# Seven half-width products for eight in the third feed-forward, and the high part of the gated product on ScalarE

## What is computed

```python
def swiglu(h, w_gu, w_down):                       # ffn2, D_FF = 2816
    a, b = jnp.split(h @ w_gu, 2, axis=-1)
    return (jax.nn.silu(a) * b) @ w_down

x = x + 0.5 * gt3[:, None, :] * swiglu(modulate(rms_norm(x, g_ffn2[l]), sh3, sc3), w2_gu[l], w2_down[l])
x = rms_norm(x, g_final)
...
h = rms_norm_2(x, ffn_norm_pre[l])                 # ffn3, D_FF_2 = 2816
y = swiglu_ffn(h, w_gate_up[l], w_down[l])         # (silu(g) * u) @ w_down
x = x + rms_norm_2(y, ffn_norm_post[l])            # the result
```

## Time and profile before

| | |
|---|---|
| median of 3 runs | 2179.72 us (2177.22 to 2183.71) |
| profiled execution | 2180.38 us, its span 2178.6 us |
| mean granted TensorE clock | 0.986 of full |
| TensorE busy | 2115.9 us (97%) |
| VectorE busy | 1297.3 us (60%) |
| ScalarE busy | 755.6 us (35%) |
| GpSimd busy | 57.1 us (3%) |

### The profile page before, as it was taken

How to read it: one execution, slowest core, us unless ns; L and a number is a source line. 1 busy time by engine, 2 the same in 40 slices (tenths; PEclk the granted TensorE clock), 3 DMA queues, 4 the chain that set the end, 5 groups by cost and what they waited for, 6 DMA issues and landing times.

```text
span 2178.6 us, 29042 instructions
## 1 busy us (share of the span) xinstructions
PE 2115.9 (97%) x11558; PEld 1769.7 (81%) x11558; DVE 1297.3 (60%) x2056; ACT 755.6 (35%) x1128; POOL 57.1 (3%) x34
## 2 busy tenths in 40 slices
PE   7999999999999999999999999998999999999998
PEld 6888888788887778788999987776688887888887
DVE  7766665644325874586877877775465465333335
ACT  4222212322323662432333354556443432212123
POOL 2000000000000000110000000000030000000000
PEclk9999999999999999999999999999999999999999
DMA  9555453222222112133222323310123122222222
GB/s 363 219 197 186 174 205 114 92 97 96 94 104 86 40 44 92 58 105 108 97 100 94 116 97 116 117 40 21 53 103 136 39 82 73 96 97 96 97 97 78
DMA packets 36452, 235.15 MB, mean 108 GB/s; under 512 B 4422, under 2 KB 6726, under 8 KB 8840
## 3 DMA queue, kind: packets, MB, share of 16 engines
q1 hardware_dynamic: 34988, 230.53, 29.1%
q10 hardware_dynamic: 1372, 3.37, 0.4%
HBM read 229.16 MB, written 4.72 MB: 107 GB/s over the span
## 4 chain that ended last, share of the span: by engine, by line
PE 86%; DVE 10%; ACT 2%; issue 1%; POOL 1%; DMA 0%; SPq 0%; DVEq 0%; ACTq 0%; POOLq 0%
PE ps L603 84%; PE ps L1018 2%; DVE w_lo L2388 1%; DVE s_lo L2396 1%; DVE ada_acc L2217 1%; ACT w_hi L1395 1%; DVE w_lo L2036 1%; DVE act_lo L2093 0%; POOL x L1989 0%; DMA ada_slot<-in_ada 0%; DVE raw L2412 0%; DVE normed L2105 0%; DVE hid_hi L2446 0%; ACT pt L1395 0%; DVE consts L2415 0%
## 5 line engine op out<-in xcount | busy, mean ns | idle before, releaser
L603 PE MATMUL ps<-act_hi,w_hi 128*128 128x512 f32 (+1 forms) x1744 | 669.4, 384 | 15.0 <-DVE s_lo L2396 4.0
L603 PE MATMUL ps<-act_lo,w_hi 128*128 128x512 f32 (+1 forms) x1744 | 658.8, 378 | 0.0
L603 PE MATMUL ps<-act_hi,w_lo 128*128 128x512 f32 (+1 forms) x1744 | 658.7, 378 | 0.0
L1395 ACT ACTIVATE w_hi<-raw 128x2048 fp32r<-128x2048 f32 (+4 forms) x205 | 340.3, 1661 | 333.6 <-PE ps L603 317.5
L603 PEld LDWEIGHTS ps<-act_hi,w_hi 128*128 128x128 f32 x1744 | 329.8, 189 | 87.1 <-issue 12.9
L603 PEld LDWEIGHTS ps<-act_hi,w_lo 128*128 128x128 f32 x1744 | 329.8, 189 | 61.2
L603 PEld LDWEIGHTS ps<-act_lo,w_hi 128*128 128x128 f32 x1744 | 330.1, 189 | 58.5 <-issue 1.0
L2036 DVE TENSOR_TENSOR w_lo<-raw,w_hi 128x2048 fp32r<-128x2048 f32 x133 | 304.9, 2293 | 62.3 <-ACT w_hi L1395 60.6
L603 PE MATMUL ps<-hid_hi,w_hi 128*128 128x512 f32 (+1 forms) x680 | 261.3, 384 | 1.7 <-DVE hid_lo L2542 1.7
L603 PE MATMUL ps<-hid_lo,w_hi 128*128 128x512 f32 (+1 forms) x680 | 260.1, 382 | 0.0
L603 PE MATMUL ps<-hid_hi,w_lo 128*128 128x512 f32 (+1 forms) x680 | 260.0, 382 | 0.0
(11 more groups left out here) (426 smaller groups left out, 2740.3 us busy)
## 6 DMA issues: line engine op xcount, KB each, us to landing
raw<-in_weights SPq DMA_DIRECT2D x176, 1024.0 KB, 4.8
ada_raw<-in_ada SPq DMA_DIRECT2D x30, 1024.0 KB, 4.9
ada_slot<-in_ada SPq DMA_DIRECT2D x6, 1024.0 KB, 14.6
bias_rows<-biasrow SPq DMA_DIRECT2D x8, 320.0 KB, 16.7
x<-in_x SPq DMA_DIRECT2D x1, 2048.0 KB, 8.2
table<-bias_rows ACTq DMA_DIRECT2D x1, 2048.0 KB, 9.2
result<-x SPq DMA_DIRECT2D x7, 256.0 KB, 2.1
consts<-in_consts SPq DMA_DIRECT2D x1, 1088.5 KB, 7.2
```

Source lines behind the costliest of these rows:

```text
L603: return nc.tensor.matmul(out, lhsT, rhs, start=start, stop=stop)
L1395: return nc.scalar.activation(out, in_, func, **kw)
```

## The change

- `ffn3` has its 18 blocks of `SEVEN` too and runs with `ffn_seven(2, ...)`. Its normed activations go to `act_full3` in place of the four `gained` buffers. The activation sums come after its second block (`turn` is 1). `ffn`'s look-ahead of one block becomes that of `ffn_seven`, two blocks.
- There is no room for all buffers: `t_hi3` lies over tiles 0 to 5 of x. ScalarE's queue copies these 1.5 MB to device memory (`kept`) once the last normed tile is there, and waits for that before it writes `t_hi3`; SP brings them back when TensorE is done with the last seven-product block, ahead of the loads of the last two weight blocks. The residual sums of the tail wait for it (`x_back`).
- `s_raw` is one buffer; `mix_weights(b)` waits for `split_lo` of b in place of b - 1. `s_lo31` lies where the second buffer was.
- `hid_hi` is written by ScalarE in both feed-forwards, after `s_hi` of b + 2 and once the product is there (`hid_high`); `hid_lo` comes after `s_lo` of b + 2 on VectorE.
- The activation sums are made by VectorE, in `ffn2` ahead of the loop, and `t_hi`, `t_lo` of `ffn2` in its first step in place of the second. GpSimd's four operations are gone.

The diff, cut to what matters (the rest hands `idx` and the buffers through):

```diff
--- before.py
+++ after.py
@@ -136,6 +136,8 @@
...
+        with ExitStack() as s:
+            t_hi3 = alloc(s, "t_hi3", [P, 3, 4, 256], F32R)
         x = sb("x", [P, DT, S])
@@ -163,6 +165,9 @@
...
+        with ExitStack() as s:
+            alloc(s, "consts_hole", [P, KAT["tri"]])
+            s_lo31 = alloc(s, "s_lo31", [P, 3, 4, P], F32R)
@@ -231,6 +236,18 @@
...
+        with ExitStack() as s:
+            alloc(s, "hid_hi_hole4", [P, 8, S]), alloc(s, "hid_lo_hole4", [P, 8, S])
+            alloc(s, "y_hole4", [P, DT, S])
+            with ExitStack() as t:
+                act_full3 = alloc(t, "act_full3", [P, DT, S])
+            t_lo3 = alloc(s, "t_lo3", [P, 3, 4, 256], F32R)
+            s_hi3 = [alloc(s, "s_hi30", [P, 3, 4, P], F32R)]
+            with ExitStack() as t:
+                t_raw3 = alloc(t, "t_raw3", [P, 3, 4, 256])
+            s_lo3 = [alloc(s, "s_lo30", [P, 3, 4, P], F32R), s_lo31]
+            s_hi3.append(alloc(s, "s_hi31", [P, 3, 4, P], F32R))
+            t1_raw3 = alloc(s, "t1_raw3", [P, 4, 256])
@@ -294,8 +311,12 @@
...
-        at = KAT["tri"]
-        s_raw = [spare[:], consts[:, at:at + 3 * S].rearrange("p (e t n) -> p e t n", e=3, t=4)]
+        s_raw = spare[:]
+        t_high_of, t_low_of = {1: t_hi, 2: t_hi3}, {1: t_lo, 2: t_lo3}
+        s_high_of, s_low_of = {1: s_hi, 2: s_hi3}, {1: s_lo, 2: s_lo3}
+        t_raw_of, t1_raw_of = {1: t_raw, 2: t_raw3}, {1: t1_raw, 2: t1_raw3}
+        full_of = {1: act_full, 2: act_full3}
+        kept = nc.dram_tensor("kept_x", (P, 6 * S), F32, kind="Internal").ap()
@@ -457,7 +479,7 @@
...
-        SEVEN = [AT["ffn2"] + 12 * third + j for third, n in enumerate(THIRDS)
+        SEVEN = [AT[name] + 12 * third + j for name in ("ffn2", "ffn3") for third, n in enumerate(THIRDS)
                  for j in range(4 if third == 0 else 0, n)]
@@ -584,9 +606,14 @@
...
-            with sp.Fori(AT["out2"] // 2, NB // 2) as p:
+            with sp.Fori(AT["out2"] // 2, NB // 2 - 1) as p:
                 for k in range(2):
                     next_load(p, k)
+            sp.wait_ge(x_kept, 16)
+            sp.wait_ge(block_done, done(SEVEN[-1]))
+            sp.dma_start(x[:, 0:6, :].rearrange("p t n -> p (t n)"), kept).then_inc(x_back, 16)
+            for k in range(2):
+                next_load(NB // 2 - 1, k)
@@ -658,15 +687,15 @@
...
                 pe.wait_ge(split_lo, b + 1)
-                pe.wait_ge(block_used, b + 1)
+                pe.wait_ge(block_used, b + 1 - offset)
...
-                pe.wait_ge(t_low, 3)
+                pe.wait_ge(t_low, 4 * idx - 1)
...
-                pe.wait_ge(t_low, 4)
+                pe.wait_ge(t_low, 4 * idx)
@@ -917,7 +946,7 @@
...
-                        if idx == 1:
+                        if idx >= 1:
                             plain = 2 if third == 0 else 0
@@ -1461,7 +1491,10 @@
...
-            def ffn_seven(b0, source):
+            def ffn_seven(idx, b0, source):
...
+                t_hi, t_raw, t1_raw = t_high_of[idx], t_raw_of[idx], t1_raw_of[idx]
+                s_hi, turn = s_high_of[idx], int(idx == 2)
...
                     p, k = divmod(b, 2)
...
                 def high_mixed(b):
                     if b in SEVEN:
                         act.wait_ge(s_step, 4 * nth(b) + 4)
-                        act.wait_ge(t_low, 3)
-                        fn(s_hi[b % 2][:], s_raw[b % 2]).then_inc(s_high, 1)
+                        act.wait_ge(t_low, 4 * idx - 1)
+                        fn(s_hi[b % 2][:], s_raw).then_inc(s_high, 1)
@@ -1489,10 +1522,11 @@
...
-                high(b0 + 1)
+                if idx == 1:
+                    high(b0 + 1)
                 for third, n in enumerate(THIRDS):
                     b = b0 + 12 * third
                     for j in range(n):
@@ -1506,8 +1540,12 @@
                         silu_of(b)
                         if more:
                             high_mixed(b + 2)
-                        if (third, j) == (0, 1):
-                            act.wait_ge(t_step, 4)
+                        act.wait_ge(block_used, used(b))
+                        fn(hid_hi[:, j, :], gu[b % 2][:, 0, :]).then_inc(hid_high, 1)
+                        if (third, j) == (0, turn):
+                            act.wait_ge(t_step, 4 * idx)
+                            if idx == 2:
+                                act.wait_ge(x_kept, 16)
                             for e in range(3):
                                 fn(t_hi[:, e], t_raw[:, e]).then_inc(t_high, 1)
                         b += 1
...
+                    elif idx == 2:
+                        token_tail(b, n)
@@ -1944,8 +1984,10 @@
...
-            prenorm()
-            ffn(AT["ffn3"], y, second_split=True, tail=True)
+            prenorm(full=act_full3)
+            act.wait_ge(x_ready, 3 * DT)
+            act.dma_start(kept, x[:, 0:6, :].rearrange("p t n -> p (t n)")).then_inc(x_kept, 16)
+            ffn_seven(2, AT["ffn3"], y)
@@ -1965,19 +2007,6 @@
...
-            early, late = token_half(0), token_half(1)
-            pool.wait_ge(full_ready, 4)
-            nc.gpsimd.tensor_tensor(t1_raw[:], act_full[:, 0:4, late], act_full[:, 0:4, early],
-                                    ALU.subtract).then_inc(t_step, 1)
-            pool.wait_ge(full_ready, DT)
@@ -2273,6 +2302,7 @@
...
                 def add_half(h, m, at, n=2):
+                    dve.wait_ge(x_back, 16)
@@ -2393,7 +2428,8 @@
                     if b in SEVEN:
                         k = b % 2
                         dve.wait_ge(s_high, nth(b) + 1)
-                        v.tensor_tensor(s_lo[k][:], s_raw[k], s_hi[k][:].bitcast(F32),
+                        dve.wait_ge(t_low, sums + (3 if b == b0 + 4 else 4))
+                        v.tensor_tensor(s_lo[k][:], s_raw, s_hi[k][:].bitcast(F32),
                                         ALU.subtract).then_inc(split_lo, 1)
...
                 def mix_weights(b):
...
-                    mixed = s_raw[k]
-                    dve.wait_ge(ms_ready, 3)
+                    mixed = s_raw
+                    dve.wait_ge(ms_ready, 3 if idx == 1 else norms[0])
                     dve.wait_ge(raw_in[k], 16 * (p + 1))
-                    dve.wait_ge(split_lo, b - 1)
+                    dve.wait_ge(split_lo, b)
...
                     v.tensor_tensor(late, gate_late.unsqueeze(1).to_broadcast([P, 2, HALF]),
...
-                def hidden(b, j):
+                def activation_sums():
+
+                    early, late = token_half(0), token_half(1)
+                    if idx == 1:
+                        dve.wait_ge(full_ready, DT)
+                    else:
+                        dve.wait_ge(normed_ready, 7 * DT)
+                    v.tensor_tensor(t1_raw[:], act_full[:, 0:4, late], act_full[:, 0:4, early],
+                                    ALU.subtract).then_inc(t_step, 1)
+                    v.tensor_tensor(t_raw[:, 1], act_full[:, 4:8, late], act_full[:, 0:4, late],
+                                    ALU.subtract).then_inc(t_step, 1)
+                    dve.wait_ge(t_step, sums + 1)
+                    v.tensor_tensor(t_raw[:, 0], act_full[:, 4:8, late], t1_raw[:],
+                                    ALU.subtract).then_inc(t_step, 1)
+                    dve.wait_ge(t_step, sums + 3)
+                    v.tensor_tensor(t_raw[:, 2], act_full[:, 4:8, early], t_raw[:, 0],
+                                    ALU.subtract).then_inc(t_step, 1)
+
+                def product(b):
                     k = b % 2
                     count["silu"] += 1
                     dve.wait_ge(silu_ready, count["silu"])
-                    if b in SEVEN:
-                        ins = v.tensor_tensor(gu[k][:, 0, :], gu[k][:, 1, :], gu[k][:, 0, :], ALU.mult)
-                    else:
-                        ins = v.tensor_tensor(gu[k][:, 0, :], gu[k][:, 1, :], ps[:, 2 * k + 1, :], ALU.mult)
-                    ins.then_inc(block_used, 1)
-                    dve.wait_ge(block_used, used(b))
-                    link(v.tensor_scalar(hid_hi[:, j, :], gu[k][:, 0, :], 1.0, None, ALU.mult))
-                    v.tensor_tensor(hid_lo[:, j, :], gu[k][:, 0, :], hid_hi[:, j, :].bitcast(F32),
+                    up = gu[k][:, 0, :] if b in SEVEN else ps[:, 2 * k + 1, :]
+                    v.tensor_tensor(gu[k][:, 0, :], gu[k][:, 1, :], up, ALU.mult).then_inc(block_used, 1)
+
+                def hidden_low(b, j):
+                    count["hid"] += 1
+                    dve.wait_ge(hid_high, count["hid"])
+                    v.tensor_tensor(hid_lo[:, j, :], gu[b % 2][:, 0, :], hid_hi[:, j, :].bitcast(F32),
                                     ALU.subtract).then_inc(hid_ready, 1)
 
-                low(b0 + 1)
+                if idx == 1:
+                    low(b0 + 1)
+                    activation_sums()
+                else:
+                    dve.wait_ge(split_lo, b0 + 2)
                 for third, n in enumerate(THIRDS):
@@ -2459,16 +2516,19 @@
```

(15 more changed lines are left out.)

38 lines of the change are left out of this document (19 added, 19 removed).

## The result

The changed kernel took **2162.24 us** (median of 4 runs, 2160.23 to 2167.41), the kernel before beside it 2181.72 us (4 runs, 2177.22 to 2185.55): ratio 0.9918, 95% interval 0.9897 to 0.9938. The forecast was 2161 us, between 2155 and 2170. The profiled executions span 2158.4 and 2178.6 us.

The account below looks back on a forecast made before the run. TensorE's order of work was taken as the clock, with VectorE's cycle delaying seven-product blocks. Terms of -6.4 us in the second feed-forward and -12.6 in the third, -19.0 together, gave 2161 us, range 2155 to 2170.

Parts of the forecast that it names:

- the fifth block's chain: Third feed-forward, first seven-product block: a 23.8 us chain from the third block against TensorE's 23.44, +0.4 us (0 to 2).
- Opening of the second feed-forward: Without GpSimd's sums, act_lo ends about 1.5 us and w_lo 0.45 us earlier: -1.95 us, capped by 2.16 us idle.
- VectorE's cycle: Seven-product blocks: s_lo to s_lo falls from 10.94 to 10.36 us, lead hides the excess; -5.8 us in second feed-forward.
- rival 1: VectorE keeps its old pace in both feed-forwards: 2172.6 us, or 2167 if half true; chance 0.13 in part or whole.
- ScalarE's copy: Seven-product blocks: ScalarE's extra 512 columns, 0.6 us, fit its 0.7 us to spare; cost zero, bounds 0 and 0.3 a block.
- Ends: Last third of both feed-forwards: w_hi of the second down block waits behind the hid_hi copy, +1.35 and +1.4 us.
- Third feed-forward: Sum there: opening 0, fifth block +0.4, 18 blocks by 0.80 us -14.4, end +1.4: -12.6 us.
- The residual tiles: Third feed-forward: 1.5 MB of x copied out and back, 7 us each, cost zero, 1.5 us to spare at the end.
- Rival 2: The copy of x makes it slower than before, above 2186 us if 41 us long; 0.05 with rival 4 and the unseen.
- rival 3: Third feed-forward: the fifth block's chain is longer than counted, lead never returns: 3 to 4 us, 2165; inside forecast's 0.76.
- Rival 4: TensorE gains nothing in the third feed-forward; excluded if VectorE holds 10.4 us; 0.05 with rival 2 and the unseen.
- rival 5: TensorE's new blocks run below 120 ns a matmul, at 109; 6 to 9 us gained, 2153; chance 0.01.

Follow-up runs that it names:

- pool_sums: The changed kernel with the four activation sums of the second feed-forward back on GpSimd: 2170.85 us (7 runs).
- before_act_copy: The kernel before with, in the second feed-forward only, ScalarE writing hid_hi and VectorE making hid_lo after s_lo: 2179.47 us, ratio 0.9996.
- no_act_copy: The changed kernel with hid_hi made by VectorE again, in the old order, in both feed-forwards: 2176.58 us, ratio to the kernel before 0.9989.
- best: Changed kernel with second feed-forward's second block split early, third's activation sums early, ScalarE's w_hi of the last thirds' second down block before silu: 2161.39 us, repeated 2160.01.
- open_early: The changed kernel with the weight split of the second feed-forward's second block made earlier on ScalarE and VectorE: 2157.27 us (one run), repeated 2160.41 us (6 runs).

## Why the prediction was right, point by point

The stretches became 6.26 + 12.63 = 18.9 us shorter, where the sum had 19.0. The mechanism held in its main terms. One small term came out by luck, that of the fifth block's chain ("Third feed-forward" below).

**Opening of the second feed-forward, -1.95.** Measured 13.36 for 15.29 us: -1.93. `pool_sums` shows the cause. Idle time stays, 2.21 us, and still ends with the `w_lo` that itself waited for ScalarE's `w_hi` (2.19 us at 917.52; the earlier trace rows had 2.20):

```profile
919.87 0.50 PE L630 MATMUL ps<-act_hi,w_hi 128*128 128x512 f32 x1 [2.21 <-DVE w_lo L2423]
```

The idle time did not shrink to below 0.5 us, against the sign that I named, and 2.16 us were no cap, since 1.93 us were won and 2.21 are left. The 2.16 us were not all of the wait: in the profile of before, the first block ran partly at half clock (mean 0.86, 13.12 of 15.29 us busy), and that filled it. `before_act_copy`, with the same opening at a clock of 1.00, has TensorE busy for 11.51 of 15.28 us. The term was right, its bound was not. The four sums on VectorE take 4.67 us behind that `w_lo` and are hidden, as expected: the second block lasts 11.06 us for 11.04.

**VectorE's cycle, 10.36.** One step of the changed kernel's last third:

```profile
2086.39 1.75 DVE L2432 TENSOR_TENSOR s_lo<-spare,s_hi 128x1536 fp32r<-128x1536 f32 x1
2088.06 0.69 DVE L2500 TENSOR_TENSOR hid_lo<-normed,hid_hi 128x512 fp32r<-128x512 f32 x1
2088.66 0.69 DVE L2445 TENSOR_TENSOR spare<-raw 128x512 f32<-128x512 f32 x1
...
2096.14 0.68 DVE L2495 TENSOR_TENSOR act<-act 128x512 f32<-128x512 f32 x1
2096.74 1.75 DVE L2432 TENSOR_TENSOR s_lo<-spare,s_hi 128x1536 fp32r<-128x1536 f32 x1
...
1993.27 1.75 DVE L2432 TENSOR_TENSOR s_lo<-spare,s_hi 128x1536 fp32r<-128x1536 f32 x1
```

2096.74 - 2086.39 = 10.35 us, the product 0.60 us to the next start where it took 0.72. It is above TensorE's 10.08 and does not show: the last `s_lo` of the third of eight is done at 1993.27 + 1.75 = 1995.02, its block starts at 1925.43 + 7 x 10.08 = 1995.99. 1.0 us of the lead was left, where 1.4 had been worked out. VectorE had no idle time between these steps (`s_lo` every 10.35 us from 1941.50 to 1993.27), against what I listed as a sign. So rival 1 fell; `no_act_copy` is the kernel in which it holds.

**ScalarE's copy, 0.** It runs behind the product, beside `s_lo`, and is done before VectorE comes to `hid_lo`, which follows `s_lo` without idle time:

```profile
2094.05 0.63 ACT L1424 ACTIVATE act<-act 128x512 f32<-128x512 f32 x1 [1.75 <-DVE act L2469]
2094.59 1.47 ACT L1424 ACTIVATE s_hi<-spare 128x1536 fp32r<-128x1536 f32 x1
2096.86 0.63 ACT L1424 ACTIVATE hid_hi<-act 128x512 fp32r<-128x512 f32 x1 [0.80 <-DVE act L2495]
```

**Ends, +1.35 and +1.4.** Measured +1.32 and +1.36, by the chain that was worked out [against rows 7]:

```profile
2114.78 0.63 ACT L1424 ACTIVATE hid_hi<-act 128x512 fp32r<-128x512 f32 x1 [0.76 <-DVE act L2495]
2115.32 1.90 ACT L1424 ACTIVATE w_hi<-raw 128x2048 fp32r<-128x2048 f32 x1
...
2117.25 2.29 DVE L2065 TENSOR_TENSOR w_lo<-raw,w_hi 128x2048 fp32r<-128x2048 f32 x1 [1.11 <-ACT w_hi L1424]
...
2119.60 0.50 PE L630 MATMUL ps<-hid_hi,w_hi 128*128 128x512 f32 x1 [1.16 <-DVE w_lo L2065]
```

`best` takes both back by moving ScalarE's `w_hi` alone ahead of the silu.

**Third feed-forward, -12.6.** The idle time ahead of its third block is 2.39 us for 2.36 (forecast 0). The 18 blocks gave 14.26 us (14.4). The fifth block came 23.98 us behind the third, forecast 23.8, before 23.44: +0.54 for +0.4. Here the sum was right by luck, by the state of one profile. Before, that pair ran partly at half clock (mean 0.93 over it); undisturbed it takes 21.86 us, as `before_act_copy` shows, whose third feed-forward is that of before. Against that the chain costs 2.1 us, not 0.4, and just more than the bound of 2 that I gave it. The stretches are then worth 17.3 us. In the changed kernel it is 23.98 us with a half-clock stretch in it (`open_early`, mean clock 0.93) and without (1.00): VectorE's chain sets it, and the slower clock fits into the wait.

**The residual tiles.** 5.1 us out and 7.6 us back, forecast 7 and 7; 3.1 us to spare at the end for the 1.5 worked out. Rival 2 would have needed 41 us for one copy.

**Rivals 3 to 5.** The chain of rival 3 is as long as counted, and its lateness costs the next four blocks no more than 0.17 us (40.48 us against 40.31). Rival 4 fell with the windows of the third feed-forward. TensorE kept 120 ns a matmul of 256 columns, so rival 5 did not come about. The 109 ns behind it are worked out from the warm gap that the Trainium skill (TensorE: Matmul & The Clock Gate, section Back-to-back issue gap) gives for a single isolated matmul; here every row is slower.

## What to carry to other kernels

Where one engine's cycle is just longer than TensorE's, sum it from start to start, with the waits for an operation's own write, and move the cheapest operation to an engine with time: 0.58 us a block on VectorE was worth 5.8 us in one feed-forward. In the other, 9.6 of the 14.3 us hung on it, together with the 0.2 us of the single buffer (`no_act_copy`). An operation given to the engine that prepares the next stage returns its cost at the last step, where nothing is left to hide it; look there for the order to undo. Judge an edit of 1 to 5 us by the distance between block starts in the trace at a known clock, or set the runs' times against their granted clock as below; the bare median hides it.
